# Thirteen turns of the last tile's expert rows moved behind the sample's front, with the sample's sixteen gathers between them

## The chip, the cores and the metric

The kernel runs on one core of a Trainium2 chip. The metric is the device time of one execution in microseconds. The kernel before has a median of 4140.63 us over three runs. The change is judged against that.

## What is computed

One layer of a hybrid decoder, in float32: paged latent attention and retention side by side, merged by gates, then a product-key expert mixer (PEER). It runs over a prompt of 1024 tokens and over a sample of 8 sequences with one new token each and 4096 cached tokens each. Cut to the part that the change touches:

```python
def peer(xn, w_q, sub_keys, expert_u, expert_v):          # per block of 128 tokens
    q = (tb @ w_q).reshape(128, 8, 2, 128); q = q * rsqrt(mean(q * q) + EPS)
    s = einsum('thpd,phkd->thpk', q, sub_keys)
    sv, si = top_k(s, 16)                                  # 16 of 128 keys, twice
    cand = sv[:, :, 0, :, None] + sv[:, :, 1, None, :]     # 256 candidates, again top 16
    ...
    g = softmax(top_s)
    act = gelu(einsum('thkd,td->thk', expert_u[eid], tb))  # 128 rows of 1024 per token
    return einsum('thk,thkd->td', g * act, expert_v[eid])

hp = hp + peer(rms_norm(hp, ffn_norm_g), ...)              # 1024 prompt tokens, 8 tiles of 128
hs = hs + peer(rms_norm(hs, ffn_norm_g), ...)              # 8 sample tokens
y_prompt, y_sample = rms_norm(hp, final_norm_g), rms_norm(hs, final_norm_g)
```

## The kernel before

The prompt is worked in T = 8 tiles of 128 tokens. For each tile there is a *front* (projections, attention, retention, merge, query products, top-k), and after it the tile's *expert rows*: 128 numbers per token, for each of which one row of `peer_u` and one of `peer_v` (4 KB each, so 128 rows, one per token, in one gather) are fetched by GpSimd with an indirect DMA. The sample's front is the ninth.

The expert rows are a stream of STEPS = 8 x 128 + 20 = 1044 steps. Step s takes the dot of row u_s with the token's vector `px` on VectorE (L2136), and adds row v_(s-20), weighted, either on VectorE (L2162, `scalar_tensor_tensor` into `xr`) or on TensorE (L1185, a product with a diagonal matrix that ScalarE makes, L2242); `on_pe` says which. The gathers (L723) alternate, u_s then v_(s-20), into a ring of nine slots `rows`; each waits until its slot's former row was consumed (`wait_row_free`). After u1023 only v rows are left (v1004 to v1023).

Two steps make one *turn*. Each engine runs the front of tile t as a generator and beside it deals turns of the stream (`beside`): 64 turns in each of the fronts 1 to 7, and 74 in the sample's front. In that last front the front has 114 yields, and `SAMPLE_SHARES` deals 17 turns over the first 14 yields (projections and the sample's retention), 35 over the next 65 (the 64 groups of cache pages), 22 over the next 32 (merge, output projection, query products, until before the last top-k). `LAST_ON_PE` = (17, 52) puts all v rows of those turns on TensorE; elsewhere odd ones are on TensorE and even ones on VectorE. So the stream of tile 7 ends before the sample's top-k, and nothing of it is left behind the front.

Behind the sample's front comes the sample's own expert part. Its 8 tokens x 8 heads x 16 experts are laid on 128 partitions x 8 columns, so it needs 8 gathers of u and 8 of v (`pool.indirect_dma_start` in L741). GpSimd issues them when the expert numbers `pe_id` are there (`p_ids`), TensorE has spread the sample's vectors (`p_spread`) and all prompt rows are consumed. VectorE copies `p_sel` (L2189), finishes prompt tile 7 (`dve_finish`: adds TensorE's sums, norm, L2175 to L2220; SP then stores it), takes eight dots (L2194), makes the coefficients; TensorE sums the eight v places (L1221), ScalarE copies the sums out (L2286) and VectorE adds and norms the sample's output (L2208 to L2220), which SP stores last. The u places were four of the ring `rows` and four of `WK`.

Each engine's instructions run in the order of its program, so what stands behind a waiting instruction on its engine waits too. Weight blocks (512 KB each) are loaded by SP into slots of `wbuf`, in the last front also of `KV`.

Of the kernel before, what the change touches and what calls it, by code (L numbers as in the profile page):

```python
# [96 lines left out]
def program(nc, a, out, const):  # L97
    _, SEQ, D = a["x_prompt"].shape
    NB = a["x_sample"].shape[0]
    _, NPHYS, PAGE, KVL = a["cache_ckv"].shape  # L100
    ROPE = a["cache_krope"].shape[3]
    _, _, RH, RDK, RDV = a["state_ret"].shape
# [5 lines left out]
    _, _, PH, NK, PD = a["peer_sub_keys"].shape  # L108
# [74 lines left out]
    with ExitStack() as ctx:  # L183
# [139 lines left out]
        p_u = [rows[:, i * D:(i + 1) * D] for i in range(4)] + [WK[:, i * D:(i + 1) * D] for i in range(4)]  # L323
# [392 lines left out]

        def pool_gathers(pool):
            for i, (kind, n) in enumerate(turns):
                t, m = divmod(n, NPAIR)
# [8 lines left out]
        def _(pool):  # L728
# [4 lines left out]

            pool.wait_ge(p_ids, 3)
            u_used.wait(pool, T - 1)
            pool.wait_ge(p_spread, 2)
            v_pe_used.wait(pool, 0, pe_before[T * NPAIR])
            v_dve_used.wait(pool, 0, dve_before[T * NPAIR])
            for table, places, arrived in ((a["peer_u"][0], p_u, p_u_in), (a["peer_v"][0], p_v, p_v_in)):
                for h in range(PH):  # L740
                    pool.indirect_dma_start(places[h], None, table, bass.IndirectOffsetOnAxis(ap=p_id[:, h:h + 1], axis=0)  # L741
                                            ).then_inc(arrived[h], 16)
# [449 lines left out]
        def _(pe):  # L1192
# [13 lines left out]
            beside(pe_front(pe, T, sample=True), experts, (NPAIR + LAG) // 2, SAMPLE_SHARES)  # L1206
# [8 lines left out]
            last.then_inc(p_spread, 1)  # L1215

# [967 lines left out]
        def dve_experts_sample(dve):  # L2184
# [5 lines left out]
            dve_finish(dve, T - 1)  # L2190
# [15 lines left out]

            dve.wait_ge(p_gathered, 1)
# [40 lines left out]
        def _(act):  # L2248
# [30 lines left out]
            beside(act_front(act, T, sample=True), experts, (NPAIR + LAG) // 2, SAMPLE_SHARES)  # L2279
            act.wait_ge(p_spread, 2)  # L2280
            nc.scalar.activation(p_x[:, :], PS[:, 512:3 * 512], ACT.Copy).then_inc(p_rows_out, 1)
            act.wait_ge(p_gelu_in, 1)
            nc.scalar.activation(p_gb, p_ga, ACT.Tanh, scale=GELU_C).then_inc(p_tanh, 1)
            act.wait_ge(p_summed, 1)
# [5 lines left out]
        def _(dve):  # L2290
# [16 lines left out]
            beside(dve_front(dve, T, sample=True), experts, (NPAIR + LAG) // 2, SAMPLE_SHARES)  # L2307
            dve_experts_sample(dve)
# [8 lines left out]
SAMPLE_SHARES = ((14, 17), (65, 35), (32, 22))  # L2317
LAST_ON_DVE, LAST_ON_PE = (74, 74), (17, 52)
# [77 lines left out]
```

## Time and profile before

| what | value |
|---|---|
| runs of the kernel before | 4140.63 us median (4137.7 to 4150.86, three runs) |
| span of the profiled execution | 4170.0 us (this is all that is shown of its time) |
| TensorE | 3270.2 us busy, 78% |
| VectorE | 2704.6 us, 65% |
| GpSimd | 2494.4 us, 60% |
| ScalarE | 739.7 us, 18% |
| DMA | 1498.19 MB, mean 359 GB/s |
| granted TensorE clock, mean | 0.912 |

Times within the profile are microseconds from the start of the span. PE is TensorE, PEld its weight loads, DVE VectorE, ACT ScalarE, POOL GpSimd, SP the engine that issues most transfers. An entry of a gather on POOL is the time in which GpSimd makes its descriptors; the rows land later. The granted clock is a share of 2.4 GHz, so 1.00 is that level and 0.50 is 1.2 GHz.

### The profile page before, as it was taken

To read this page: it belongs to the slowest core of one execution; us is meant where nothing else is said; L and a number is where in the kernel's file an instruction comes from. 1 tells how busy PE (TensorE), PEld (TensorE's weight loads), DVE (VectorE), ACT (ScalarE), POOL (GpSimd) and SP (SyncE) were. 2 spreads that over 40 slices of the span, in tenths; PEclk is the share of its full clock that TensorE was granted. 3 is DMA by queue.
4 is the path that set the end of the run, shared out by engine and by line. 5 is a ranking of instruction groups with operands and counts; after the bars stand their busy time and mean duration, and the time that the engine had idled before them with its cause. 6 is when DMAs were issued, how large, how long until landed. Compare 5 with 4: busy or idle time off the path is not lost.

```text
span 4170.0 us, 39232 instructions
## 1 busy us (share of the span) xinstructions
PE 3270.2 (78%) x11253; PEld 1605.8 (39%) x11253; DVE 2704.6 (65%) x6214; ACT 739.7 (18%) x2273; POOL 2494.4 (60%) x2069
## 2 busy tenths in 40 slices
PE   7877877767888877867988777877898777799854
PEld 3334333332344332423444333433353323466532
DVE  2156568766876578766876577657875686655544
ACT  2112111220112111211121022202131120211111
POOL 0005766777666767776666667666667675544452
PEclk9998999988999999889989999999999997899976
DMA  5668999999999999999999999999999999999996
GB/s 184 219 225 301 402 391 400 353 403 381 398 372 376 403 395 343 365 402 402 384 369 398 402 371 364 382 402 398 390 389 398 397 349 346 327 320 323 327 387 232
DMA packets 580362, 1498.19 MB, mean 359 GB/s; under 512 B 90506, under 2 KB 147475, under 8 KB 580147
## 3 DMA queue, kind: packets, MB, share of 16 engines
q0 software_dynamic: 297216, 1082.26, 67.8%
q1 hardware_dynamic: 242850, 401.10, 26.7%
q10 hardware_dynamic: 40082, 12.32, 1.2%
q8 instruction: 92, 1.51, 0.1%
q14 instruction: 122, 1.00, 0.1%
HBM read 1485.33 MB, written 10.13 MB: 359 GB/s over the span
## 4 chain that ended last, share of the span: by engine, by line
PE 35%; DMA 24%; POOL 16%; issue 11%; DVE 10%; ACT 3%; another core or an unknown queue 1%; ACTq 0%; SPq 0%; DVEq 0%; POOLq 0%
POOL rows L723 15%; DMA rows<-in_peer_v_dram,pe_id 14%; PE PS L1185 12%; PE PS L818 11%; DMA rows<-in_peer_u_dram,pe_id 4%; PE PS L1102 3%; DVE rows L2136 3%; PE PS L827 2%; DMA wbuf<-in_w_in_dram 2%; DMA wbuf<-in_peer_w_q_dram 2%; DMA wbuf<-in_w_out_dram 2%; PE PS L783 1%; DVE xr L2162 1%; PE PS L963 1%
## 5 line engine op out<-in xcount | busy, mean ns | idle before, releaser
L723 POOL DMA_INDIRECT rows<-in_peer_u_dram,pe_id x1024 | 1241.3, 1212 | 919.7 <-PE PS L1185 308.9
L1185 PE MATMUL PS<-rows,diags 128*128 128x512 f32 x2544 | 1357.0, 666 | 457.4 <-DMA rows<-in_peer_v_dram,pe_id 394.8
L723 POOL DMA_INDIRECT rows<-in_peer_v_dram,pe_id x1024 | 1233.8, 1205 | 697.0 <-DVE dots L2136 379.1
L2136 DVE CUSTOM_DVE_ANT_0 rows<-rows,px 128x1024 f32<-128x1024 f32 x1024 | 1242.2, 1223 | 503.0 <-DMA rows<-in_peer_u_dram,pe_id 477.7
L1185 PEld LDWEIGHTS PS<-rows,diags 128*128 128x128 f32 x2544 | 490.8, 208 | 1105.4 <-issue 987.6
L818 PE MATMUL PS<-wbuf,xt 128*128 128x512 f32 (+1 forms) x1696 | 781.1, 597 | 81.4 <-DMA wbuf<-in_w_in_dram 38.3
L2162 DVE SCALAR_TENSOR_TENSOR xr<-rows,gcoef,xr 128x1024 f32<-128x1024 f32 x388 | 498.4, 1285 | 158.9 <-issue 146.5
L818 PEld LDWEIGHTS PS<-wbuf,xt 128*128 128x128 f32 x1696 | 322.1, 197 | 510.4 <-issue 364.2
L818 PE MATMUL PS<-wbuf,wide 128*128 128x512 f32 (+1 forms) x736 | 344.8, 610 | 37.4 <-ACT wide L1292 15.2
L2242 ACT ACTIVATE diags<-ident,gcoef 128x128 f32<-128x128 f32 x636 | 231.1, 399 | 203.7 <-PE PS L1185 81.7
L818 PEld LDWEIGHTS PS<-wbuf,wide 128*128 128x128 f32 x736 | 145.1, 202 | 221.8 <-issue 163.2
L783 PE MATMUL PS<-ident,WK 128*128 128x128 f32 x572 | 96.5, 313 | 93.4 <-DVE WK L1855 51.2
L827 PE MATMUL PS<-wbuf,KV 128*128 128x512 f32 (+1 forms) x352 | 156.0, 565 | 0.0
L783 PEld LDWEIGHTS PS<-ident,WK 128*128 128x128 f32 x572 | 79.0, 162 | 141.5 <-DVE WK L1855 58.8
L1281 ACT ACTIVATE z<-PS 128x512 f32<-128x512 f32 (+1 forms) x60 | 32.8, 567 | 474.5 <-PE PS L827 188.8
L963 PE MATMUL PS<-KV,WK 128*128 128x64 f32 x576 | 83.1, 293 | 30.0 <-ACT WK L1436 25.6
L1281 ACT ACTIVATE WK<-PS 128x512 f32<-128x512 f32 x42 | 25.1, 597 | 433.3 <-PE PS L818 328.3
L943 PE MATMUL PS<-KV,qt 96*128 96x512 f32 (+3 forms) x192 | 79.1, 522 | 26.6 <-DVE mx L1804 23.2
L827 PEld LDWEIGHTS PS<-wbuf,KV 128*128 128x128 f32 x352 | 65.7, 190 | 77.0 <-issue 77.0
L963 PEld LDWEIGHTS PS<-KV,WK 128*128 128x128 f32 x576 | 74.3, 203 | 45.9 <-ACT WK L1436 33.3
L1804 DVE CUSTOM_DVE_ANT_0 WK<-PS,WK 128x128 f32<-128x128 f32 (+7 forms) x64 | 48.2, 754 | 56.6 <-PE PS L943 53.6
L1431 ACT ACTIVATE WK<-WK,nmx 128x128 f32<-128x128 f32 (+7 forms) x64 | 49.5, 774 | 198.2 <-DVE nmx L1808 173.6
(374 smaller groups left out, 2665.6 us busy)
## 6 DMA issues: line engine op xcount, KB each, us to landing
wbuf<-in_w_in_dram SPq DMA_DIRECT2D x278, 512.0 KB
wbuf<-in_peer_w_q_dram SPq DMA_DIRECT2D x136, 512.0 KB
wbuf<-in_w_out_dram SPq DMA_DIRECT2D x68, 512.0 KB
wbuf<-in_w_ob_dram SPq DMA_DIRECT2D x66, 512.0 KB
wbuf<-in_w_oa_dram SPq DMA_DIRECT2D x36, 512.0 KB
rows<-in_peer_u_dram,pe_id POOLq DMA_INDIRECT x1028, 4.3
rows<-in_peer_v_dram,pe_id POOLq DMA_INDIRECT x1024
KV<-in_cache_ckv_dram SPq DMA_DIRECT2D x128, 128.0 KB
```

Of the source, the lines that this page charges most:

```text
L723: pool.indirect_dma_start(row_slot(kind, n), None, a["peer_u" if kind == "u" else "peer_v"][0], bass.IndirectOffsetOnAxis(ap=pe_id[t % 2][ ...
L783: last = nc.tensor.transpose(b[0:m, k * n:(k + 1) * n], src, ident[0:n, 0:n])
L818: last = nc.tensor.matmul(bnk, lhs[:, (k0 + j) * P:(k0 + j + 1) * P], block_w[:, j * wd:(j + 1) * wd], start=(k0 + j == 0), stop=(n == n0 ...
L827: last = nc.tensor.matmul(other, next_lhs(t, k0 + j), block_w[:, j * wd:(j + 1) * wd], start=(k0 + j == 0), stop=(n == n0 + slots - 1 and ...
L943: last = nc.tensor.matmul(DD.bank(tj, "score", h)[:, i:i + w], qt[0:HD, h * P:(h + 1) * P], key_t[0:HD, h, i:i + w], start=True, stop=True)
L963: last = nc.tensor.matmul(bank[6][:, h * VH:(h + 1) * VH], pt[:, k * P:(k + 1) * P], value[:, k, h * VH:(h + 1) * VH], start=(k == 0), sto ...
L1102: last = nc.tensor.matmul(PS[:, at_:at_ + P], qsc[b % 2][:, k * P:(k + 1) * P] if k < 8 else qsc_rope[b % 2], blocks_of[:, k] if k < 8 els ...
L1185: last = nc.tensor.matmul(bank[3 + 4 * c], diag(n), row_slot("v", n)[:, c * 512:(c + 1) * 512], start=start, stop=stop)
L1281: return nc.scalar.activation(dst[:, at_:at_ + wd], b[:, 0:wd], func, scale=scale)
L2136: V.tensor_tensor_reduce(out=row, in0=row, in1=px[:, :], scale=1.0, scalar=0.0, op0=ALU.mult, op1=ALU.add, accum_out=dots[:, at_:at_ + 1]) ...
L2162: V.scalar_tensor_tensor(out=y[:, :], in0=row_slot("v", n), scalar=gcoef[:, g % 2 * TOPK + k:g % 2 * TOPK + k + 1], in1=y[:, :], op0=ALU.m ...
L2242: nc.scalar.activation(diag(n), ident[:, :], ACT.Copy, scale=gcoef[:, g % 2 * TOPK + k:g % 2 * TOPK + k + 1]).then_inc(diag_ready.sem, 1)
```

## The change

- 61 turns instead of 74 are dealt beside the sample's front: 15, 29 and 17 instead of 17, 35 and 22. `LAST_ON_PE` becomes (15, 45), again the turns of the pages.
- The other 13 turns (`REST` = (3, 10)) follow the front: on VectorE and ScalarE three before the sample's dots and tanh and ten after the sample's coefficients; on TensorE all 13 between the spreading of the sample's vectors and the sample's sums.
- GpSimd issues the sample's sixteen gathers within the stream, ahead of the gather of v1005. Its waits for all prompt rows to be consumed go.
- The sample's u places move from `rows` to `wbuf`.
- `dve_finish` of tile 7 moves behind the last ten turns.

```diff
-        p_u = [rows[:, i * D:(i + 1) * D] for i in range(4)] + [WK[:, i * D:(i + 1) * D] for i in range(4)]
+        p_u = [wbuf[:, i * D:(i + 1) * D] for i in range(4)] + [WK[:, i * D:(i + 1) * D] for i in range(4)]
...
+        def pool_sample_gathers(pool):
+            pool.wait_ge(p_ids, 3)
+            pool.wait_ge(p_spread, 2)
+            for table, places, arrived in ((a["peer_u"][0], p_u, p_u_in), (a["peer_v"][0], p_v, p_v_in)):
+                for h in range(PH):
+                    pool.indirect_dma_start(places[h], None, table, bass.IndirectOffsetOnAxis(ap=p_id[:, h:h + 1], axis=0)
+                                            ).then_inc(arrived[h], 16)
+
         def pool_gathers(pool):
             for i, (kind, n) in enumerate(turns):
+                if i == turn_of["v", STEPS - 2 * sum(REST) + 7 - LAG]:
+                    pool_sample_gathers(pool)
...
             pool_gathers(pool)
-
-            pool.wait_ge(p_ids, 3)
-            u_used.wait(pool, T - 1)
-            pool.wait_ge(p_spread, 2)
-            v_pe_used.wait(pool, 0, pe_before[T * NPAIR])
-            v_dve_used.wait(pool, 0, dve_before[T * NPAIR])
-            for table, places, arrived in ((a["peer_u"][0], p_u, p_u_in), (a["peer_v"][0], p_v, p_v_in)):
-                for h in range(PH):
-                    pool.indirect_dma_start(places[h], None, table, bass.IndirectOffsetOnAxis(ap=p_id[:, h:h + 1], axis=0)
-                                            ).then_inc(arrived[h], 16)
...
-            beside(pe_front(pe, T, sample=True), experts, (NPAIR + LAG) // 2, SAMPLE_SHARES)
+            beside(pe_front(pe, T, sample=True), experts, (NPAIR + LAG) // 2 - sum(REST), SAMPLE_SHARES)
...
             last.then_inc(p_spread, 1)
+            for _ in range(sum(REST)):
+                next(experts)
 
             pe.wait_ge(p_built, 5)
...
-        def dve_experts_sample(dve):
+        def dve_experts_sample(dve, experts):
...
             link(dve, V.tensor_copy(p_sel, bank[0][:, 0:NB]))
-            dve_finish(dve, T - 1)
+            for _ in range(REST[0]):
+                next(experts)
             dve.wait_ge(p_rows_out, 1)
...
                             spread(p_coef, PH, NB), ALU.mult).then_inc(p_built, 1)
 
+            for _ in range(REST[1]):
+                next(experts)
+            dve_finish(dve, T - 1)
             dve.wait_ge(p_gathered, 1)
...
             nc.scalar.activation(p_x[:, :], PS[:, 512:3 * 512], ACT.Copy).then_inc(p_rows_out, 1)
+            for _ in range(REST[0]):
+                next(experts)
             act.wait_ge(p_gelu_in, 1)
             nc.scalar.activation(p_gb, p_ga, ACT.Tanh, scale=GELU_C).then_inc(p_tanh, 1)
+            for _ in range(REST[1]):
+                next(experts)
             act.wait_ge(p_summed, 1)
...
-SAMPLE_SHARES = ((14, 17), (65, 35), (32, 22))
-LAST_ON_DVE, LAST_ON_PE = (74, 74), (17, 52)
+SAMPLE_SHARES = ((14, 15), (65, 29), (32, 17))
+REST = (3, 10)
+LAST_ON_DVE, LAST_ON_PE = (74, 74), (15, 45)
```

## Rows read from the trace of the kernel before

**Rows 1.** Busy time of each engine in five stretches of the end, all instructions.

```profile
core 0: us, PE busy (x) PEld busy (x) DVE busy (x) ACT busy (x) POOL busy (x), PEclk, DMA share, GB/s
3449.00:3599.00 150.00, 95.57 (x316) 45.95 (x314) 97.81 (x220) 23.13 (x82) 82.35 (x69) 0.75 0.95 339
3599.00:3934.00 335.00, 309.40 (x2039) 218.07 (x2043) 198.56 (x364) 52.04 (x174) 157.77 (x141) 0.97 0.97 328
3934.00:4088.00 154.00, 93.00 (x899) 49.19 (x895) 69.53 (x107) 26.18 (x91) 73.97 (x59) 0.75 0.97 368
4088.00:4131.00 43.00, 29.11 (x335) 16.17 (x330) 15.39 (x63) 13.94 (x73) 4.18 (x5) 0.81 0.40 150
4131.00:4170.00 39.00, 7.95 (x64) 1.30 (x64) 23.19 (x65) 1.71 (x5) 18.00 (x16) 0.50 0.63 230
```

**Rows 2.** Waits, 3599 to 3934: who waited for whom, total us, times, longest.

```profile
DVE KV L2075 <- PE PS L1102: 85.3, 25, 7.4
```

**Rows 3.** Waits, 3934 to 4131.

```profile
PE PS L1185 <- DMA rows<-in_peer_v_dram,pe_id: 19.9, 4, 11.3
```

**Rows 4.** Timeline, VectorE at 4130: start, duration, operation.

```profile
4130.27 0.36 DVE L2015 CAST pe_id<-i 32x8 uint32<-32x8 f32 x2
...
4132.25 1.28 DVE L2175 TENSOR_TENSOR xr<-xr,PS 128x512 f32<-128x512 f32 x2
...
4137.32 1.28 DVE L2220 SCALAR_TENSOR_TENSOR xr<-xr,fin,final_gain 128x1024 f32<-128x1024 f32 x1
```

**Rows 5.** Timeline, GpSimd's gathers for the sample (five of sixteen).

```profile
4130.89 0.94 POOL L741 DMA_INDIRECT rows<-in_peer_u_dram,pe_id  x1 [37.33 <-DVE pe_id L2015]
...
4138.51 0.94 POOL L741 DMA_INDIRECT WK<-in_peer_u_dram,pe_id  x1 [0.31 <-issue]
4139.75 1.97 POOL L741 DMA_INDIRECT WK<-in_peer_u_dram,pe_id  x1 [0.30 <-issue]
...
4148.87 0.98 POOL L741 DMA_INDIRECT KV<-in_peer_v_dram,pe_id  x1 [0.31 <-issue]
...
4152.63 0.94 POOL L741 DMA_INDIRECT xt<-in_peer_v_dram,pe_id  x1 [0.30 <-issue]
```

**Rows 6.** Timeline, from the last of the sample's eight sums on.

```profile
4158.90 1.04 PE L1221 MATMUL PS<-xt,decays 128*8 128x256 f32 x8 [0.20 <-DMA xt<-in_peer_v_dram,pe_id]
4160.00 1.54 ACT L2286 ACTIVATE wide<-PS 8x256 f32<-8x256 f32 x4 [10.11 <-PE PS L1221]
4161.57 1.21 DVE L2208 TENSOR_TENSOR xr<-xr,wide 8x1024 f32<-8x1024 f32 x1 [10.96 <-ACT wide L2286]
```

**Rows 7.** Timeline, a dot that frees a slot and the gather that waited.

```profile
3578.57 1.22 DVE L2136 CUSTOM_DVE_ANT_0 rows<-rows,px 128x1024 f32<-128x1024 f32 x1
...
3580.07 1.74 POOL L723 DMA_INDIRECT rows<-in_peer_v_dram,pe_id  x1 [12.68 <-DVE dots L2136]
```

**Rows 8.** Timeline, v rows, on TensorE at the lower clock and on VectorE.

```profile
4065.79 3.78 PE L1185 MATMUL PS<-rows,diags 128*128 128x512 f32 x4
...
4067.75 2.69 DVE L2162 SCALAR_TENSOR_TENSOR xr<-rows,gcoef,xr 128x1024 f32<-128x1024 f32 x2
```

**Rows 9.** The page's part 3, the queue of all gathers: packets, MB, share.

```profile
q0 software_dynamic: 297216, 1082.26, 67.8%
```

**Rows 10.** Gathers of the stream alone (L723) in the first stretch.

```profile
3449.00:3599.00 150.00, 82.35 (x69) 0.75 0.95 339
```

**Rows 11.** Waits, 3450 to 3600.

```profile
POOL rows L723 <- DVE dots L2136: 29.8, 4, 12.7
...
DVE KV L2062 <- DMA KV<-in_state_ret_dram: 9.5, 1, 9.5
```

**Rows 12.** TensorE's v rows alone (L1185) in the stretch of the pages.

```profile
3599.00:3934.00 335.00, 129.97 (x276) 51.06 (x276) 0.97 0.97 328
```

**Rows 13.** Timeline, SP's last query weights and the last query block.

```profile
4091.50 7.58 SPq L563 DMA_DIRECT2D wbuf<-in_peer_w_q_dram  x4
...
4114.39 1.08 PE L814 MATMUL PS<-wbuf,xt 128*32 128x128 f32 x32
```

More of the change, by code:

```diff
@@ L2278, in _ @@
                 beside(act_front(act, t), experts, NPAIR // 2)
-            beside(act_front(act, T, sample=True), experts, (NPAIR + LAG) // 2, SAMPLE_SHARES)
+            beside(act_front(act, T, sample=True), experts, (NPAIR + LAG) // 2 - sum(REST), SAMPLE_SHARES)
             act.wait_ge(p_spread, 2)
             nc.scalar.activation(p_x[:, :], PS[:, 512:3 * 512], ACT.Copy).then_inc(p_rows_out, 1)
+            for _ in range(REST[0]):
+                next(experts)
             act.wait_ge(p_gelu_in, 1)
             nc.scalar.activation(p_gb, p_ga, ACT.Tanh, scale=GELU_C).then_inc(p_tanh, 1)
+            for _ in range(REST[1]):
+                next(experts)
             act.wait_ge(p_summed, 1)
@@ L2306, in _ @@
             V.memset(oret, 0.0).then_inc(s_zero, 1)
-            beside(dve_front(dve, T, sample=True), experts, (NPAIR + LAG) // 2, SAMPLE_SHARES)
-            dve_experts_sample(dve)
+            beside(dve_front(dve, T, sample=True), experts, (NPAIR + LAG) // 2 - sum(REST), SAMPLE_SHARES)
+            dve_experts_sample(dve, experts)
         third = len(checkpoints) // 3
```

## The prediction

> **What bounds the kernel now.** I read the stage table first [rows 1], for stretches that I cut at the sample's own work: its projections and retention (3449 to 3599 us), its 64 groups of cache pages (3599 to 3934), merge, output projection and query weights (3934 to 4131), and the tail. Up to 4088 the DMA engines are 95 to 97% busy, and in the page stretch TensorE is busy for 309.4 of 335 us at nearly full clock; so that stretch has two limits close together. There VectorE's page transposes wait 85.3 us for TensorE [rows 2], which makes TensorE the nearer one. In the last stretch TensorE is busy for 122 of 197 us and waits for gathered rows [rows 3]: that one goes by transfers and by latency. After 4088 DMA falls to 40%: the chain through four query blocks, top-k and the cast of the expert numbers runs with the memory nearly idle.
>
> The tail starts when the expert numbers are there, at X = 4130.27 + 0.36 = 4130.6 [rows 4]. Its limit is GpSimd's queue: sixteen gathers, the first starting at 4130.89, the last at 4152.63, 1.45 us apart on average [rows 5]. The last one's rows reach TensorE at 4158.90, 6.2 us after its issue started; eight sums end at 4160.0, ScalarE copies for 1.54, and VectorE's norm and the store run from 4161.57 to the end of the span, 4170.0 [rows 6]. So X to end is 39.4 us. VectorE's finish of prompt tile 7 (4132.2 to 4138.6) and its eight dots lie beside the gathers and cost nothing.
>
> **What the change moves.** 61 turns instead of 74 are dealt over the last front (15, 29, 17 instead of 17, 35, 22). The 13 held back are steps 1018 to 1043: six dots (u1018 to u1023) and 26 weighted rows (v998 to v1023), odd ones on TensorE, even ones on VectorE. The sample's sixteen gathers are put before the gather of v1005, and 19 row gathers follow them.
>
> **Tail, step by step** (times after X). GpSimd's ring has nine slots. The list of gathers goes u1018, v998, u1019, v999 and so on up to u1022, v1002, u1023, v1003, v1004; each waits for the one nine places ahead. With 61 turns consumed it can have issued everything through u1022; v1002 needs the slot of u1018, u1023 that of v998, v1003 that of u1019, v1004 that of v999. These four stand in the queue ahead of the sample's, and u1018 is read by VectorE only after the whole front and the copy of p_sel, at 1.6, where the finish of tile 7 starts in before [rows 4]. A dot that frees a slot starts its gather 1.50 later, and that gather then takes 1.74 [rows 7]. So v1002 goes out at 3.1, u1023 at 5.1, v1003 at 6.4, v1004 at 7.6, the sample's first at 8.9 instead of 0.3. Sixteen at 1.45 bring v1005 to 32.1. VectorE meanwhile does six dots and three rows (6 x 1.22 + 3 x 1.28 = 11.2 [rows 7, 8]), waits a little for u1023 and is through at 13; the sample's dots go as they land, the coefficients are ready at about 28: hidden. The 19 rows behind go while VectorE is mostly idle, at 1.25 to 1.42 apart as in the last eight of before [rows 5]; I take 1.30: v1023 starts at 32.1 + 18 x 1.30 = 55.5 and lands at 61.7.
>
> TensorE's order is the new wait: the sample's sums stand behind all 13 turns. In before the sums ran as the rows landed, and only the last came after the last landing; now all eight come after v1023. TensorE's clock in the tail is 0.50, the 1.2 GHz level, after long idling [rows 1], and a weighted row then costs 3.78 [rows 8]: done at 65.5. Eight sums at 1.04 [rows 6] give 8.3: 73.8. ScalarE's copy with its start 1.6, then the same 8.4 of VectorE and store: 83.8. The finish of tile 7 needs v1023, takes 6.4 [rows 4] and runs from 65.5 to 71.9, under the sums; if they were at full clock it would end last and cost 2 to 3. SP's store of that tile moves from 4138.6 to just after it, under the final norm. ScalarE's diagonals stand around the sample's tanh: those of v1008 on wait until about 28, their rows land after 42. Moving p_u from rows to wbuf costs nothing: the last query weights are consumed before p_spread.
> Tail: 83.8 - 39.4 = **44.4 us more**. Low end: every gather 1.25 apart, TensorE at full clock (1.9 per row, half the sums): 34. High end: 1.5 to 1.72 apart: 50.
>
> **Front, given back.** Nothing of these shorter stretches is in the trace, so each is bounded. One gather is 1082.26 MB / 2064 = 0.524 MB [rows 9].
> - Projections and retention: two turns, eight gathers fewer than the 69 [rows 10]. If DMA is the limit, 8 x 0.524 MB at 339 GB/s [rows 1] = 12.4 us; if VectorE's order is, 2 x (2 x 1.22 + 1.28) = 7.4 [rows 7, 8]; where a state load sets the pace (9.5 us of waiting [rows 11]), 4 or less. I take 8.
> - Pages: six turns, all on TensorE, twelve rows of 129.97 / 69 = 1.88 [rows 12]: 22.6. If DMA is the limit, 24 gathers at 328 GB/s: 38. I take 24, near TensorE's figure, because of the waits above.
> - Last stretch: 17 instead of 22 turns, but the last ten of before have no dots, so about 68 gathers are consumed either way. Up to the first query block (24 of 32 deals) 6 fewer are issued: 6 x 0.524 at 368 GB/s = 8.5 if DMA sets the pace. Behind it some 17 come where 5 did [rows 1]; they fill idle DMA. SP issues its last query weights by 4099.1 and the last query block runs at 4114.4 [rows 13], so the weights have some slack against them, but may give some back. Between 0 and 8.5 I take 5.
> Front: 8 + 24 + 5 = **37 us less**, bounds 27 and 59. What shortens each stretch next is the other limit (DMA in the pages), which is why I don't add the ends.
>
> Sum: 44.4 - 37 = +7.4. The profile's span of 4170.0 would become 4177.4 (no more than the span is shown of that execution); the median of the runs is 29 us below it, so 4140.6 + 7.4 = **4148 us**.
>
> **The rivals.**
> A, forecast, 0.42: as above, its own range 4138 to 4158 (5 either way on both sides).
> B, slower, 0.22: only TensorE's time in the pages comes back, because the other stretches go by chains of latency. Then 44.4 - 22.6 = +22: 4162. For it: GpSimd idles 29.8 us for dots in the first stretch, behind front work in VectorE's order [rows 11]; against it: DMA at 95% there. It ends slower wherever the front gives back less than 32 us.
> C, faster, 0.14: DMA is the limit all through the front, and each gather that leaves it pays its full transfer: 12.4 + 38 + 8.5 = 59, net -15: 4126. For it: 0.97 busy in the pages; against it: the waits for TensorE.
> D, 0.10: the four gathers are not stuck (VectorE reaches u1018 before its lists end), and the sample's gathers start at X. Then 8.6 less: 4139. Against it: the dealt turns come after the last top-k step in VectorE's program.
> E, 0.07: gathers that start under a VectorE dot are held until it ends. The trace has this: 0.94 became 1.97 for the one started at 4139.75, in a dot [rows 5], and under the eight dots the pitch was 1.72 (six steps in 10.4 us). Twenty gathers at 1.72 add 5.4, and ten of the rows behind, each held 1.03 by a VectorE row, add 10: 4164. I give it little since in before the dots cover only half of the gathers' time. The Trainium skill, SBUF — State Buffer, section "SBUF: two separate sides", says that GpSimd can't write descriptors while VectorE holds the port pair they share, an exclusive lock; by that rule the price is E's, by the average spacing it is A's. The long gathers agree with the rule, the short ones in the same stretch do not show it.
> The rest, 0.05, is spread.
>
> **Range and chances.** 4125 to 4165 reaches from C's time to beyond B and E; it leaves out about 0.1 on each side. A measurement of this kernel tells 0.3% (12.4 us) from no change, so faster means below 4128 and slower above 4153. Faster: most of C and a little of the tails, 0.16. Same: most of A, D, a little of C, 0.52. Slower: B, E and the upper part of A, 0.32.
>
> **What would show it.** In the changed profile: four row gathers between the cast of pe_id and the first gather into wbuf, the latter 8 to 9 us after the cast (D if at once); 19 row gathers behind the sample's, 24 us; from the cast to the end 84 us; the pages' stretch about 311 us with TensorE still over 90% busy (C if near 297); the first stretch about 142 us. The prediction is wrong if the front gives back less than 32 or more than 56 us, or if the sample's sums don't wait for the last row.

## The result, and the profile after

The changed kernel takes 4156.74 us (median of 12 runs, 4143.47 to 4164.2), the kernel before, run beside it, 4142.4 (12 runs, 4133.73 to 4150.86). The ratio of the two is 1.0028 with a 95% interval of 1.0015 to 1.0042, which is 11.6 us slower; the medians alone differ by 14.3. So it is slower, the interval lying above 1, by about the 0.3% (12.4 us) that the prediction took for the limit of no change. Forecast were 4148 us and +7.4. Below, a ratio turned into us is the ratio times the kernel before, and differs from the difference of the medians by up to 3 us.

The page's head, span and busy time of the engines:

```profile
span 4151.3 us, 39187 instructions
...
PE 3240.0 (78%) x11233; PEld 1596.4 (38%) x11233; DVE 2711.8 (65%) x6219; ACT 737.9 (18%) x2268; POOL 2516.3 (61%) x2069
```

The stretches: projections and retention, pages, last stretch, tail. The columns are those of [rows 1], but one cut is not: here, and in all that follows, the pages end with the first matmul of L1166, behind the last page's sums, which in the kernel before is at 3940.5, while [rows 1] cuts at 3934. Its pages are 341.6 us long by this cut and 335 by that one. The two pieces of the last stretch are one here.

```profile
3441.10:3581.80 140.70, 85.69 (x307) 41.68 (x306) 90.19 (x205) 24.57 (x89) 68.24 (x62) 0.75 0.93 328
3581.80:3889.70 307.90, 289.96 (x2045) 209.54 (x2046) 185.34 (x342) 46.90 (x156) 129.83 (x116) 0.97 0.97 324
3889.70:4073.70 184.00, 115.12 (x1162) 62.26 (x1163) 89.21 (x181) 39.27 (x161) 88.80 (x72) 0.73 0.94 358
4073.70:4151.30 77.60, 29.15 (x110) 10.42 (x108) 47.66 (x96) 4.77 (x15) 40.68 (x39) 0.70 0.71 271
```

TensorE's rows of v alone (L1185) in the pages, beside [rows 12], and the waits there, beside [rows 2]:

```profile
3581.80:3889.70 307.90, 106.40 (x228) 42.18 (x228) 0.97 0.97 324
```
```profile
DVE KV L2077 <- PE PS L1102: 95.1, 46, 5.5
```

In the pages TensorE is busy for 290 of 308 us, 94%, and VectorE's transposes still wait for it, more often than before. The tail went from 39.4 to 77.6 us; GpSimd makes 39 gathers in it where [rows 1] has 16. The three stretches before it are 632.6 us together, where the one execution of before had 681.8. That difference of 49 can't be the gain in the runs, since 38.2 more in the tail would then leave a faster kernel: the profiled execution of before was itself some 28 us above the median of its runs, and this one is not (4153.11 us, 3.6 under its median). The part ahead of these stretches, which the change leaves alone, was 7.7 us longer in it as well (3448.8 against 3441.1). The experiments below are there to size the gain within one set of runs.

The tail, gather by gather. This is GpSimd's timeline from the cast of the expert numbers, which ends at X = 4073.7: start, duration, operation, idle time before it and what ended that.

```profile
4076.66 1.74 POOL L733 DMA_INDIRECT rows<-in_peer_v_dram,pe_id  x1 [13.68 <-DVE dots L2138]
4078.71 1.98 POOL L733 DMA_INDIRECT rows<-in_peer_u_dram,pe_id  x1 [0.31 <-issue]
4080.99 0.94 POOL L733 DMA_INDIRECT rows<-in_peer_v_dram,pe_id  x1 [0.30 <-issue]
4082.23 1.97 POOL L733 DMA_INDIRECT rows<-in_peer_v_dram,pe_id  x1 [0.30 <-issue]
4084.50 0.94 POOL L722 DMA_INDIRECT wbuf<-in_peer_u_dram,pe_id  x1 [0.30 <-issue]
...
4095.74 0.97 POOL L722 DMA_INDIRECT KV<-in_peer_v_dram,pe_id  x1 [0.30 <-issue]
...
4104.89 0.94 POOL L733 DMA_INDIRECT rows<-in_peer_v_dram,pe_id  x1 [0.30 <-issue]
...
4127.99 0.94 POOL L733 DMA_INDIRECT rows<-in_peer_v_dram,pe_id  x1 [0.30 <-issue]
```

Four gathers of the stream stand ahead of the first one into `wbuf`, as forecast; the first waited for the dot that frees its slot. The sample's sixteen take 20.4 us (1.27 apart), the 19 of the rows behind follow at 1.28, and none of the 35 waits for a slot. GpSimd's undisturbed pace is 1.24 (0.94 of work and 0.30 to the next); what lies above it are gathers that took longer. The end of the tail, from the timelines of TensorE, VectorE, ScalarE and SP:

```profile
4134.56 1.95 PE L1185 MATMUL PS<-rows,diags 128*128 128x512 f32 x4 [0.56 <-DMA rows<-in_peer_v_dram,pe_id]
4136.44 3.21 PE L1223 MATMUL PS<-KV,decays 128*8 128x256 f32 x56
4139.47 0.61 PE L1223 MATMUL PS<-xt,decays 128*8 128x256 f32 x8
...
4140.15 1.54 ACT L2296 ACTIVATE wide<-PS 8x256 f32<-8x256 f32 x4 [22.79 <-PE PS L1223]
...
4143.01 0.36 SPq L616 DMA_DIRECT2D out_y_p_dram<-xr  x1
4149.04 0.32 SPq L616 DMA_DIRECT2D out_y_s_dram<-xr  x1
```

First the last row of v, then all eight sums (they stand behind the last row, as forecast). But row and sums run at twice the forecast speed, and VectorE's finish of tile 7 (4136.6 to 4143.0, stored at 4143.01) now ends after ScalarE's copy (4141.7). TensorE's rows of v alone (L1185) in pieces of the tail show the clock: columns are its busy time and number of matmuls, its weight loads, granted clock, DMA share, GB/s.

```profile
4100.00:4111.00 11.00, 0.00 (x0) 0.00 (x0) 0.50 1.03 410
4111.00:4118.00 7.00, 6.59 (x12) 2.87 (x12) 0.71 1.02 407
4118.00:4136.00 18.00, 13.75 (x30) 4.74 (x28) 1.00 0.87 347
```

TensorE had no row between 4100 and 4111 and was at 0.50 (1.2 GHz), then worked off three rows almost without a pause (6.59 of 7 us), and from 4118 was granted 1.00 (2.4 GHz) and kept it with one row per 2.5 us.

### The profile page after: what moved, and what is told of

The parts are those of the page before. It is cut to its first block and busy times, and to the rows that moved or that the text cites. A ratio compares the mean times of both kernels' runs of the same rounds, so it can differ in the third digit from the quotient of the medians.

```text
span 4151.3 us, 39187 instructions
## 1 busy us (share of the span) xinstructions
PE 3240.0 (78%) x11233; PEld 1596.4 (38%) x11233; DVE 2711.8 (65%) x6219; ACT 737.9 (18%) x2268; POOL 2516.3 (61%) x2069
## 5 line engine op out<-in xcount | busy, mean ns | idle before, releaser
L1185 PE MATMUL PS<-rows,diags 128*128 128x512 f32 x2524 | 1344.0, 665 | 491.7 <-DMA rows<-in_peer_v_dram,pe_id 453.8
L733 POOL DMA_INDIRECT rows<-in_peer_v_dram,pe_id x1024 | 1252.7, 1223 | 685.6 <-DVE dots L2138 408.7
L1185 PEld LDWEIGHTS PS<-rows,diags 128*128 128x128 f32 x2524 | 487.2, 208 | 1139.9 <-issue 991.2
L818 PE MATMUL PS<-wbuf,wide 128*128 128x512 f32 (+1 forms) x736 | 341.4, 605 | 36.7 <-ACT wide L1294 14.8
L1849 DVE TENSOR_TENSOR xr<-PS,xr 128x512 f32<-128x512 f32 x16 | 11.1, 691 | 112.5 <-PE PS L818 112.5
```

Of the source, the lines that this page charges most:

```text
L733: pool.indirect_dma_start(row_slot(kind, n), None, a["peer_u" if kind == "u" else "peer_v"][0], bass.IndirectOffsetOnAxis(ap=pe_id[t % 2][ ...
L818: last = nc.tensor.matmul(bnk, lhs[:, (k0 + j) * P:(k0 + j + 1) * P], block_w[:, j * wd:(j + 1) * wd], start=(k0 + j == 0), stop=(n == n0 ...
L1185: last = nc.tensor.matmul(bank[3 + 4 * c], diag(n), row_slot("v", n)[:, c * 512:(c + 1) * 512], start=start, stop=stop)
```

## The experiments

"X" is the end of the cast of the expert numbers, "tail" is X to the end of the span. Ratios are to the kernel before, run beside them on the same chip. The kernel before had three medians in the three sets: 4183.3 (set 1: before_again, hold6_pages, hold7_ends, sample_first), 4142.0 (set 2: after_again, unstuck, hold7_split, hold9_split) and 4170.8 (set 3: before_third, hold7_ends_2, hold7_split_2, hold4_ring). So stretches are compared within a set only. All stretches in one table, us:

```
                 set  first  pages  last   tail   ratio
before            -   150.1  341.6  190.1  39.4
after             -   140.7  307.9  184.0  77.6   1.0028
before_again      1   155.4  341.2  190.4  39.2   0.9995
sample_first      1   148.0  321.8  182.5  83.1   1.0014
hold6_pages       1   150.8  322.1  203.5  53.3   1.0008
hold7_ends        1   141.5  339.5  182.0  55.7   0.9997
after_again       2   145.3  307.5  183.3  80.6   1.0042
unstuck           2   140.6  307.7  181.8  77.0   1.0035
hold7_split       2   140.4  315.2  175.5  48.6   0.9954
hold9_split       2   142.6  311.3  193.3  55.3   1.0014
before_third      3   154.7  338.8  190.4  39.0   0.9984
hold7_ends_2      3   152.9  334.4  182.9  54.6   1.0001
hold7_split_2     3   151.6  338.5  183.4  49.2   0.9974
hold4_ring        3   147.6  338.2  189.4  40.9   0.9977
```

**The kernel before, twice more.**

> The kernel before, unchanged, to learn how far two profiles of one program differ. In the profile before the change the sample's front took 681.8 us (memset of oret at 3448.8 to the cast of the expert numbers ending at 4130.6), in the changed kernel's 632.6: 49 us given back, while the tail from the cast to the end grew by 38.2 (39.4 to 77.6) and the timed runs say +12 in all. Theory: the front gave back only about 27 and the profile before was a slow one; then this profile has a front of about 660 and a tail of 39. Rival: it gives back 49 and something else, outside the last front, costs 23; then this front is again 682. Time against the kernel before: 1.000.

> The kernel before in the same call as the next three, so that stretches of its profile stand beside theirs from one chip. Front 667 to 687 us, tail 39, ratio 1.000.

Measured: 0.9995 [0.998, 1.001] and 0.9984 [0.9963, 1.0005]. Both include 1. The second compares the kernel before with itself and comes out 0.16% off, so a ratio of set 3 that is only a little further from 1 says little. The theory in the first text was a miss: it took the first profile for a slow one and expected a front (the three stretches before the tail) of about 660 us. The front was 687.0 here and 683.9 in before_third, so 681.8 was no outlier; but in these sets the whole kernel takes longer too, so this does not settle what the change gained. The tail and the last stretch repeat within 0.4 us, while the first stretch moved by 5 and the pages by 3 between executions.

**The change, once more.**

> The changed kernel again, for a second profile and a second ratio. Two profiles of the kernel before have fronts of 682 and 687 us; the changed kernel's first had 633, and a variant with the same front 652. Theory: the front gives back about 30 (a front near 653) and the tail costs 38, so the ratio is 1.002 to 1.003. Rival: the first profile is typical, the front 633 and the ratio below 1.

Measured: 1.0042 [1.0026, 1.0059], 17 us slower, tail 80.6. Neither text fits whole: the front was 636.1 us, near the rival's 633, and the ratio lies above the theory's 1.002 to 1.003. The change is slower than before in both measurements, and by something between 0.15 and 0.6%.

The 3.0 us between the two tails lie in GpSimd's queue. The last gather starts at X + 57.4 here and at X + 54.3 in the first profile, and the 39 gathers took 43.9 us of GpSimd's time instead of 40.7, with the same pause of 0.30 between them. Some of the long ones, under the sample's dots and under a row on VectorE that began at 4117.99:

```profile
4094.82 1.60 POOL L722 DMA_INDIRECT WK<-in_peer_u_dram,pe_id  x1 [0.30 <-issue]
...
4118.12 1.97 POOL L733 DMA_INDIRECT rows<-in_peer_v_dram,pe_id  x1 [0.30 <-issue]
```

**The sample's end ahead of the last ten turns (sample_first).** Same turns and same front as the change; only what stands behind them is reordered:

```diff
-            sp_store_y(sp, T - 1)
-            sp_store_y(sp, T, NB)
+            y_ready.wait(sp, T - 1)
+            sp.dma_start(out["y_s"].rearrange("b s d -> (b s) d"), xr[T % 2][0:NB, :]).then_inc(y_stored, 16)
+            y_ready.wait(sp, T)
+            sp.dma_start(out["y_p"][0][ds((T - 1) * P, P), :], xr[(T - 1) % 2][:, :]).then_inc(y_stored, 16)
...
-            for _ in range(sum(REST)):
+            for _ in range(REST[0]):
...
             last.then_inc(p_summed, 1)
+            for _ in range(REST[1]):
+                next(experts)
...
-            for _ in range(REST[1]):
+            for _ in range(4):
                 next(experts)
-            dve_finish(dve, T - 1)
...
+            for _ in range(REST[1] - 4):
+                next(experts)
+            dve_finish(dve, T - 1)
```

So TensorE does three turns, the sample's sums, ten turns; VectorE four of the ten turns, the sample's norm, the other six, and the finish of tile 7 last; SP stores `y_s` ahead of `y_p`.

> The changed kernel with another order behind the front: TensorE's sums for the sample before the last ten turns, VectorE's norm and SP's store of the sample after four of the ten, the finish of tile 7 last. In the changed kernel VectorE does the finish (6.3 us) and then the sample's norm and store (8.4) after the last row. Theory: the order costs what stands behind the last row, so the tail falls from 77.6 by 8.4 less a store of 512 KB instead of 32 KB (3 more): -5, ratio to before about 1.0015 where the change has 1.0028. Rival: the big store at the end takes as long as it saves: no change, 1.0028.

Measured: 1.0014 [1.0001, 1.0028]; the ratio was expected, the tail was not: 83.1 us instead of some 73. That the ratio came out right is luck. The three stretches of the front in before_again:

```profile
3457.10:3612.50 155.40, 97.12 (x316) 46.24 (x314) 97.90 (x220) 23.16 (x81) 80.42 (x69) 0.74 0.92 325
3612.50:3953.70 341.20, 314.38 (x2093) 222.04 (x2094) 198.43 (x364) 52.91 (x177) 157.99 (x141) 0.96 0.98 329
3953.70:4144.10 190.40, 117.01 (x1171) 62.10 (x1171) 84.78 (x168) 39.49 (x162) 78.04 (x63) 0.76 0.84 320
```

And in sample_first:

```profile
3458.30:3606.30 148.00, 90.36 (x308) 42.62 (x306) 90.20 (x205) 24.40 (x88) 69.31 (x61) 0.73 0.90 311
3606.30:3928.10 321.80, 295.82 (x2044) 213.02 (x2044) 184.84 (x342) 47.14 (x157) 130.90 (x117) 0.96 0.93 310
3928.10:4110.60 182.50, 118.68 (x1163) 63.10 (x1163) 88.36 (x182) 39.36 (x161) 90.72 (x72) 0.77 0.95 361
```

TensorE's rows of v alone (L1185, here L1187) in the pages, of before_again and then of sample_first:

```profile
3612.50:3953.70 341.20, 129.12 (x276) 50.54 (x276) 0.96 0.98 329
```
```profile
3606.30:3928.10 321.80, 107.50 (x228) 42.56 (x228) 0.96 0.93 310
```

This is the one pair of profiles in which before and the change's front ran in one set: 7.4 + 19.4 + 7.9 = 34.7 us less, where 8 + 24 + 5 = 37 was predicted. The twelve rows of v that left the pages took 21.6 us of TensorE with them (129.12 - 107.50), TensorE's whole busy time fell by 18.6, and the stretch by 19.4. The DMA rate fell with it, from 329 to 310 GB/s, instead of staying up: in this pair the pages' time goes with TensorE's, not with the transfers.

The order did save what it was meant to: from the end of the last row to the end of the span it is 9.6 us here and 14.8 in the change. But the tail did not shrink, because TensorE's sums ran slowly. The timeline of TensorE (L1225 are the sums), and then of ScalarE, VectorE and GpSimd:

```profile
4156.18 1.34 PE L1225 MATMUL PS<-KV,decays 128*8 128x256 f32 x3 [0.81 <-issue]
4156.95 0.61 PE L1225 MATMUL PS<-xt,decays 128*8 128x256 f32 x2
```
```profile
4158.84 1.54 ACT L2302 ACTIVATE wide<-PS 8x256 f32<-8x256 f32 x4 [16.86 <-PE PS L1225]
...
4160.41 1.21 DVE L2217 TENSOR_TENSOR xr<-xr,wide 8x1024 f32<-8x1024 f32 x1 [3.05 <-ACT wide L2302]
...
4161.73 1.43 POOL L735 DMA_INDIRECT rows<-in_peer_v_dram,pe_id  x1 [8.05 <-PE PS L1187]
```

From 4143.9 to 4158.7 TensorE did half of the sums, 32 of 64 matmuls in 14.8 us, with pauses that the profile puts down to nothing ("issue"), while the DMA share was 0.98. The rows behind them waited, so their slots stayed full, and GpSimd stood still for 8.05 us. Gathers that took long added 7.5 us over the 39, where the first profile of the change has 4.0. Why the sums were slow was not settled. In the change's order all eight took 3.6 us behind the last row, with DMA nearly idle. But full DMA alone does not slow them: in hold7_split (below) five of the eight took 4.6 us at a DMA share of 1.02 and a granted clock of 0.50:

```profile
4087.10 4.58 PE L1225 MATMUL PS<-KV,decays 128*8 128x256 f32 x40 [17.08 <-DVE decays L2211]
```

**Part of the change alone: six turns out of the pages (hold6_pages), seven out of the two ends (hold7_ends).**

```diff
-SAMPLE_SHARES = ((14, 15), (65, 29), (32, 17))
-REST = (3, 10)
-LAST_ON_DVE, LAST_ON_PE = (74, 74), (15, 45)
+SAMPLE_SHARES = ((14, 17), (65, 29), (32, 22))
+REST = (0, 6)
+LAST_ON_DVE, LAST_ON_PE = (74, 74), (17, 46)
```
```diff
-SAMPLE_SHARES = ((14, 15), (65, 29), (32, 17))
-REST = (3, 10)
-LAST_ON_DVE, LAST_ON_PE = (74, 74), (15, 45)
+SAMPLE_SHARES = ((14, 15), (65, 35), (32, 17))
+REST = (0, 7)
+LAST_ON_DVE, LAST_ON_PE = (74, 74), (15, 50)
```

> Only the six turns of the cache pages held back (17, 29, 22 dealt; last six turns, all v rows, behind the front; same tail order otherwise). The ring can run nine gathers ahead, so of the twelve held rows only five are gathered behind the sample's sixteen: last row issued at 26 us after the cast, landed at 33, finish of tile 7 and sample's norm behind it: tail about 49 to 50 instead of 39, +10. If the pages give back TensorE's time for twelve rows (22.6 us): -12, ratio 0.997. If they go by DMA (34 to 38 us): -25, ratio 0.994. If the front gives nothing: +10, 1.0025.

> The complement: two turns fewer in the first stretch and five fewer in the last, the pages as before (15, 35, 17; seven turns behind the front). Tail: seven gathers behind the sample's, about 52, +12.5. By the changed kernel's profile the two stretches gave 9.4 and 6.1: -3, ratio 0.9993. If they go by chains of latency and give 0 to 4 (rival B): +9 to +12, ratio 1.0025.

Measured: 1.0008 [0.9992, 1.0023], a miss, and 0.9997 [0.9983, 1.0011], as expected. The tails of both were longer than expected, 53.3 instead of 49 to 50 and 55.7 instead of 52: the gathers under the sample's dots took up to 1.88, and all together 4.8 and 5.0 us more than 0.94 each. hold6_pages did save 19.1 us in the pages. Its last stretch gave 13 back, here against before_again's row above (190.40 us, 63 gathers on GpSimd):

```profile
3939.00:4142.50 203.50, 123.42 (x1175) 64.23 (x1175) 99.61 (x197) 40.07 (x164) 106.19 (x82) 0.77 0.92 350
```

The number of u rows is fixed. A turn dealt late shifts the whole stream, so that the last 22 turns of this kernel hold 36 dots and 44 rows of v, 80 gathered blocks, where before's last 22 hold 24 and 44 = 68 (its last ten turns had no dots). Over the kernels more blocks go with more time, though the groups overlap: 62 blocks with 175.5 to 183.4 us, 68 with 181.8 to 190.4, 74 with 193.3, 80 with 203.5. In set 1 that is (203.5 - 190.4) / 12 = 1.1 us a block from before_again and (203.5 - 182.5) / 12 = 1.75 from sample_first, which also has 68. A block's transfer is 0.524 MB at 368 GB/s = 1.4 [rows 1, 9], between the two. That the blocks are the cause is argued from this count; no run changed them alone. The change itself has 68 there, as the prediction counted.

**The four stuck gathers (unstuck).** The sample's gathers go ahead of v1002 instead of v1005, and all 13 turns stand behind the coefficients on VectorE:

```diff
-                if i == turn_of["v", STEPS - 2 * sum(REST) + 7 - LAG]:
+                if i == turn_of["v", STEPS - 2 * sum(REST) + 4 - LAG]:
...
-REST = (3, 10)
+REST = (0, 13)
```

> The changed kernel with the sample's gathers put before the gather of v1002 and all 13 turns behind the sample's coefficients, so that nothing stands ahead of the sample's gathers that waits for a dot (rival D made true). Theory: the four gathers that were stuck cost their waiting, not only their place: the first sample gather starts 0.3 after the cast instead of 10.8, the last row's gather at about 49 instead of 54.3, and the tail falls by 5: ratio about 1.0015. Rival: the tail is the number of gathers times their spacing, and only the start (3 us) is won: 1.002.

Measured: 1.0035 [1.002, 1.005] beside 1.0042 of after_again; expected were 1.0015 by the theory and 1.002 by the rival; the rival is the nearer, at the edge of the interval. Its timeline has the first sample gather 0.3 us after its X of 4070.1, and the last row's:

```profile
4070.36 0.94 POOL L722 DMA_INDIRECT wbuf<-in_peer_u_dram,pe_id  x1 [11.82 <-DVE pe_id L2017]
...
4123.76 0.94 POOL L733 DMA_INDIRECT rows<-in_peer_v_dram,pe_id  x1 [0.30 <-issue]
```

The sample starts 10.5 us earlier after X than in the change, and the last row's gather only 0.6 (X + 53.7 against X + 54.3), or 3.7 against after_again (X + 57.4), the run beside it: the tail is 77.0 against 77.6 and 80.6. The four gathers are not lost by standing first, they are part of the same queue: 39 gathers follow X in all three kernels. Only the 2.7 us by which the queue starts earlier are won by this order, as the rival said. Against the change's first profile 2.1 of them were lost again to gathers that took longer, such as this one, which began within a dot (4079.03 to 4080.18):

```profile
4079.19 1.87 POOL L722 DMA_INDIRECT WK<-in_peer_u_dram,pe_id  x1 [0.30 <-issue]
```

So the last gather starts at X + the start of the first + 1.24 for each one before it + what the long ones took beyond 0.94. For the change that is 3.0 + 38 x 1.24 + 4.0 = 54.1 (54.3), for after_again 3.0 + 47.1 + 7.2 = 57.3 (57.4), for unstuck 0.3 + 47.1 + 6.1 = 53.5 (53.7).

The expectation says that this makes rival D true. It does not: D has the four gathers out before X, so that 35 follow it, and here they are moved behind the sample's. No run tests D.

**Seven or nine turns held back, the sample's end among them (hold7_split, hold9_split).** The order of sample_first, the sample's gathers ahead of everything that would be stuck, fewer turns:

```diff
-                if i == turn_of["v", STEPS - 2 * sum(REST) + 7 - LAG]:
+                if i == turn_of["v", STEPS - 2 * sum(REST) + 9 - LAG]:
...
-SAMPLE_SHARES = ((14, 15), (65, 29), (32, 17))
-REST = (3, 10)
-LAST_ON_DVE, LAST_ON_PE = (74, 74), (15, 45)
+SAMPLE_SHARES = ((14, 15), (65, 35), (32, 17))
+REST = (4, 3)
+LAST_ON_DVE, LAST_ON_PE = (74, 74), (15, 50)
```

hold9_split has (65, 31), (32, 19), REST = (4, 5) and (15, 46) in their place. The turns between the coefficients and the sample's norm on VectorE are two of three, and four of five.

> Seven turns held back, from the first and last stretch as in hold7_ends (0.9997, tail 55.7), but only what the ring can't fetch ahead is left behind the sample's gathers (five), four turns are worked while the sample's rows are on their way, TensorE sums the sample before the last three, and the sample's norm and store come before the finish of tile 7. Theory: the tail's price is what stands behind the last row; it falls from 55.7 to about 48, ratio 0.998. Rival: TensorE's sums under full DMA run as slowly as in the kernel with the sample first (13 us instead of 3.6) and nothing is won: 0.9997.

> The same with nine turns held back (15, 31, 19 dealt), four of them pages' turns. Nine gathers behind the sample's; last row issued at 32 us, landed at 38.5, finish and store behind it: tail about 51, +11.5. If the front gives back in proportion to the gathers taken out of it (9, against 5 in hold7_split), 22 us or more: ratio 0.9975 or less. If it gives what rows on TensorE in the pages cost, and hands two thirds of it to the last stretch as in hold6_pages: 20 us, 0.998.

Measured: hold7_split 0.9954 [0.9938, 0.9969], 4119.81 us against 4142.0; hold9_split 1.0014 [1.0002, 1.0027]. The first gained more than the 0.998 expected, at the tail expected (48.6). The second is a miss: its last stretch holds 74 blocks and took 193.3 us against 175.5, which fits hold6_pages, and its tail was 55.3 instead of 51. hold7_split's end on TensorE, and then SP's two stores:

```profile
4095.33 1.03 PE L1225 MATMUL PS<-xt,decays 128*8 128x256 f32 x8 [0.24 <-DMA xt<-in_peer_v_dram,pe_id]
...
4101.77 1.95 PE L1187 MATMUL PS<-rows,diags 128*128 128x512 f32 x4 [0.56 <-DMA rows<-in_peer_v_dram,pe_id]
```
```profile
4105.28 0.32 SPq L709 DMA_DIRECT2D out_y_s_dram<-xr  x1
4112.88 0.36 SPq L711 DMA_DIRECT2D out_y_p_dram<-xr  x1
```

The last sum ends at the sample's last landing, its norm lies beside the last rows, and only the finish of tile 7 and its store stand behind the last row: 12.3 us from that row's end (4103.7) to the end of the span, where the change has 14.8 (4136.5 to 4151.3). Here the sums were not slow. Its pages, with the 35 turns of before:

```profile
3576.70:3891.90 315.20, 306.07 (x2092) 215.40 (x2092) 199.69 (x371) 50.41 (x167) 157.32 (x141) 0.98 1.03 355
```

**The same two orders side by side (hold7_ends_2, hold7_split_2).**

> hold7_ends once more, beside its split version on one chip. The two differed by 0.43% (0.9997 and 0.9954, in different calls), of which the tails explain 7 us (55.7 to 48.6), 0.17%. Theory: the order behind the front is the only thing that differs, so the gap in one call is 7 to 9 us, 0.2%. Rival: the order also makes the front shorter, and the gap is again 18 us.

> hold7_split once more. By the theory 7 to 9 us under hold7_ends_2, ratio 0.9955 to 0.998; tail 48 to 49. By the rival 0.9954 with hold7_ends_2 at 0.9997.

Measured: 1.0001 [0.9985, 1.0017] and 0.9974 [0.9962, 0.9985], tails 54.6 and 49.2. The order is worth 0.27%, 11 us with some 8 either way, of which the tail shows 5.4: the last gather starts 3.2 earlier (two fewer, and fewer long ones), and 2.2 are won behind it, where the norm no longer stands behind the last row. The expected 7 to 9 fit; the rival's 18 lies at the edge of what the times allow, but its reason does not show, since the front of hold7_split_2 was not shorter (673.5 against 670.2 us). The gain of hold7_split over before appears in both sets, at 0.46% (five runs) and 0.26% (eight runs); the second is not far beyond the 0.16% by which before_third differs from itself in that set.

**Only what the ring holds (hold4_ring).** Four turns are held back; their rows are gathered ahead into the ring before X, and the sample's gathers follow the whole stream.

```diff
-                if i == turn_of["v", STEPS - 2 * sum(REST) + 7 - LAG]:
-                    pool_sample_gathers(pool)
...
             pool_gathers(pool)
+            pool_sample_gathers(pool)
...
-SAMPLE_SHARES = ((14, 15), (65, 29), (32, 17))
-REST = (3, 10)
-LAST_ON_DVE, LAST_ON_PE = (74, 74), (15, 45)
+SAMPLE_SHARES = ((14, 15), (65, 35), (32, 20))
+REST = (4, 0)
+LAST_ON_DVE, LAST_ON_PE = (74, 74), (15, 50)
```

> Only four turns held back (15, 35, 20 dealt), eight v rows, all of which the ring of nine slots fetches before the sample's gathers; they are worked while the sample's rows are on their way, and the finish of tile 7 under the wait for the sample's sums. Theory: what the ring has fetched costs the tail nothing (39 to 41) and the front still gives back two turns of the first stretch (7 to 9 us) and a little of the last, where the number of gathers consumed stays 68: ratio 0.997 to 0.9985. Rival: give-back goes by the gathers that leave the front, of which there are none here: 1.000.

Measured: 0.9977 [0.9964, 0.9991], as expected, though again close to before_third's own 0.9984. Its first sample gather starts 0.3 us after X (4128.0) and the last takes its place at 4150.64, as in before:

```profile
4128.26 0.94 POOL L722 DMA_INDIRECT wbuf<-in_peer_u_dram,pe_id  x1 [15.95 <-DVE pe_id L2016]
...
4150.64 0.94 POOL L722 DMA_INDIRECT xt<-in_peer_v_dram,pe_id  x1 [0.30 <-issue]
```

The four turns cost the tail 1.9 us (40.9 against 39.0). The first stretch gave back 7.1 (147.6 against 154.7), but hold7_ends_2 and hold7_split_2, with the same 15 turns there, gave back 1.8 and 3.1, so what two turns of it are worth is not known to a few us. With no gather of a row behind X the move is nearly free.

## Why the prediction held, and where its steps were off

The sign held, and so did the shape: a tail that grows by some 40 us and a front that gives back less than that. The tail was priced too dear and the front too generously, and the two errors partly cancelled.

- **Tail: 83.8 predicted, 77.6 measured** (80.6 in the second run). By steps, measured against predicted: first sample gather X + 10.8 against 8.9, since two of the four stuck ones took 1.97 where about 1.0 was taken; the sixteen 20.4 against 23.2; the rows' 18 spacings 23.1 against 23.4; landing and start of the last row 6.6 against 6.2; that row 1.95 against 3.78; all behind it 14.8 against 18.3. The last two are one mistake: **"TensorE's clock in the tail is 0.50, after long idling"** was read from a tail in which TensorE had eight short sums to do [rows 1]. With some ten rows to do it was granted 1.00. The sentence that the finish of tile 7 "would end last and cost 2 to 3" at full clock is what happened: 6.4 of finish behind the row, then the sample's 8.4.
- **The stuck gathers: the account was right, and the price somewhat low.** They put the sample's first gather at X + 10.8. Of this 3.0 is the wait for the first dot and 7.8 the place of four gathers in the queue. unstuck removes only the wait, and its tail is 0.6 us shorter than the change's first one and 3.6 shorter than after_again's, run beside it. The 7.8 would be saved only if the four went out before X, which is rival D; its 4139 stays untested. hold4_ring, where all rows are fetched before X, shows at least that such gathers cost the tail little.
- **Front: 37 predicted.** One pair in one set gives 34.7. First stretch 8: measured 7.4 there, but the five profiles of sets 1 and 3 with these 15 turns, beside before's in the same set, range from 1.8 to 13.9. Last stretch 5: measured 7.9. Pages 24: measured 19.4, near TensorE's figure as argued, but below even its 22.6, because TensorE's other busy time there grew by 3. In time the front gave back what the tail grew less the loss measured: 38.2 - 11.6 = 27 for the change, 41.2 - 17.4 = 24 for after_again and 37.6 - 14.5 = 23 for unstuck, but 43.9 - 5.9 = 38 for sample_first, each with some 6 us either way. Where the kernel before took 4183 the 37 is met, where it took 4142 it is 10 to 14 too high. The prediction called itself wrong if the front gave back less than 32: by these times it did so in three of four cases, so **the front's 37 is the term that was mis-sized**, and by its own sign this step failed although the time held.
- **Why the pages give back more in one set than in another stays open.** In set 2 the pages with 35 turns (hold7_split) took 315.2 us at 355 GB/s, with 31 turns (hold9_split) 311.3 and with 29 (after_again) 307.5, so that six turns were worth only 7.7 there. TensorE was 97% busy in the first of these and the DMA share 1.03, so both were near their limit. Set 2 has no profile of the kernel before, so that this is a lead and no more.
- **Rival C** (DMA the bound, 59 given back, faster) fell: the kernel is slower, and in set 1 the transfer rate drops when turns leave the pages. Comparing the first two profiles alone (49 less) would have spoken for it. **Rival B**'s time is the nearer one (4162; measured 4156.7, and 17 us slower in after_again), but not wholly for its reason: in set 1 the other two stretches did shorten, by 7 and 8, and the pages gave 5 less than predicted.
- **Rival E** (gathers held under VectorE): three of the first four gathers show it, at 1.74, 1.98 and 1.97 instead of 0.94, while the sixteen of the sample and the 19 behind were 0.93 to 1.22. Over 39 gathers that is 4.0 us, and 7.2 in after_again; the spacing of 1.45 from before, which the sum used for the sixteen, already held some of it. So E's mechanism is there, but smaller than E had it.
- **The signs named beforehand** were there in part: first stretch 142 (140.7), TensorE over 90% busy in the pages (94%), four row gathers ahead of the first one into `wbuf`, 19 behind the sample's in 24 us (23.1 to the start of the last). The first gather into `wbuf` came 10.8 us after the cast instead of 8 to 9, and cast to end was 77.6 instead of 84. The pages, 311 by the cut of [rows 1], were 307.9 by the cut used here; without the 6.5 us between the cuts that is about 301, nearer to C's 297 than to 311, in a pair of profiles that overstates the gain.
- **Slower by 11.6 us instead of 7.4:** a tail 6 cheaper and a front some 10 poorer. That is within the range, and by luck in part.

## What to carry to other kernels

Count the queue that ends last: behind X the time was the start of the first gather, 1.24 us for each one after it, 1.8 to 7.5 us for gathers that took longer than 0.94, and what stands behind the last one. Another order of the same gathers won only the wait at its start (2.7 us); fewer gathers, or moving work from behind the last one to beside it, won more. Holding back what a ring of buffers can fetch ahead costs the tail nearly nothing (four turns, 1.9 us), each turn beyond it two gathers, 2.5 us or more; and a stream that is shifted later carries its expensive steps into the next stretch, so look where the dots go and not only where the turns go. The version that took seven turns from the two ends, left the pages alone and put the sample's sums and norm ahead of the last rows is faster than the kernel before, by 0.46% and 0.26% in two sets, and 0.9% faster than the change where both were run side by side.

## What the runs showed of the hardware

A gather is held by a VectorE operation that is under way, and not the other way round. VectorE's timeline in the change's tail:

```profile
4078.65 1.22 DVE L2138 CUSTOM_DVE_ANT_0 rows<-rows,px 128x1024 f32<-128x1024 f32 x1
...
4079.79 1.28 DVE L2164 SCALAR_TENSOR_TENSOR xr<-rows,gcoef,xr 128x1024 f32<-128x1024 f32 x1
...
4094.68 1.23 DVE L2197 CUSTOM_DVE_ANT_0 wbuf<-wbuf,wide 128x1024 f32<-128x1024 f32 x1
4095.82 0.08 DVE L2197 DVE_READ_ACCUMULATOR2_ANT decays<- 128x1 f32 x1
```

The gather that started at 4078.71, 0.06 us into the dot, took 1.98: the usual 0.94 and 1.04 more, which reaches to 4079.75, where the dot ended (VectorE's next entries begin at 4079.79). The row of 4079.79 started when that gather still had most of its own work to do, and took its usual 1.28. Under the sample's dots of this profile gather and dot fell into step: gathers came 1.28 apart, each starting just before a dot ended (4095.74 against 4095.82), so each took 0.03 longer only. These rows do not make that a rule: under the same eight dots in after_again gathers took up to 1.60. The Trainium skill, SBUF — State Buffer, section "SBUF: two separate sides", calls the shared port pair an exclusive lock that whoever starts first holds for the whole instruction. The first half of that agrees with the 1.98; the second, that VectorE would be blocked in turn, these rows do not show.

The other two surprises are the granted clock, which rose to 1.00 and stayed there with TensorE busy 1.95 of every 2.5 us, and the sums of sample_first, which took 14.8 us for half of them, where all took 3.6 in the change and five of eight took 4.6 in hold7_split with DMA as full. The first is shown, the cause of the second is not.
